# Keys, values and tables made ahead of the layers and behind V, in a two-layer hybrid decoder trunk

## What is computed

```python
for l in range(DEPTH):
    h = rmsnorm(x, norm_mix[l])
    ...   # projections; o_hg, o_s5, o_rt; gates; merge
    x = x + merged @ w_out[l]
    x = x + cross_attn(rmsnorm(x, norm_cross[l]), rmsnorm(mem, norm_mem[l]), xa_wq[l], xa_wkv[l], xa_wo[l])
    x = x + peer(rmsnorm(x, norm_ffn[l]), peer_wq[l], peer_keys[l], peer_u[l], peer_v[l])
# in cross_attn, mem_n = rmsnorm(mem, norm_mem[l]):
    k, v = jnp.split(mem_n @ wkv, 2, axis=-1)
# in s5, the tables: functions of the parameters alone
    dt = jnp.exp(log_step)[:, None]; mag = jnp.exp(lr * dt)
    a_re = mag * jnp.cos(li * dt); a_im = mag * jnp.sin(li * dt)
    bb_re = z_re[..., None] * b_re - z_im[..., None] * b_im
    bb_im = z_re[..., None] * b_im + z_im[..., None] * b_re
```

## Time and profile before

| | |
|---|---|
| median of 3 runs | 5575.65 us (5574.95 to 5576.41) |
| the profiled execution | 5575.93 us, its span 5574.1 us |
| TensorE busy | 4937.0 us, 89% of the span |
| VectorE busy | 2640.8 us, 47% |
| ScalarE busy | 1656.7 us, 30% |
| GpSimd busy | 290.5 us, 5% |
| DMA queue of SP | 717.58 MB, 39.1% of 16 engines' span |

### The profile page before, as it was taken

The page is one execution under the profiler, slowest core; times in us unless marked ns, Lnnn a source line. Parts: engine busy times, 40 slices in busy tenths (PEclk is TensorE's granted clock), DMA queues, the critical chain, the costliest instruction groups (busy, mean ns, idle before and its releaser), DMA issues. The chain is left out here.

```text
span 5574.1 us, 57335 instructions
## 1 busy us (share of the span) xinstructions
PE 4937.0 (89%) x23352; PEld 4085.8 (73%) x23352; DVE 2640.8 (47%) x4121; ACT 1656.7 (30%) x2116; POOL 290.5 (5%) x96
## 2 busy tenths in 40 slices
PE   7986387888999999999989765877799999999998
PEld 5765366666888888888877644665688888888887
DVE  2236743269744424444422466432796444244444
ACT  2232123232333322222232322232233333222222
POOL 0002300002100000000000122000030000000000
PEclk9998688998999999999999976888899999999999
DMA  2220032023455556666522101331144555566665
GB/s 109 91 95 16 12 132 98 31 80 118 136 189 183 182 170 192 199 188 197 170 107 95 76 16 23 121 113 46 50 135 151 181 176 183 183 186 199 192 193 164
DMA packets 308469, 721.24 MB, mean 129 GB/s; under 512 B 18544, under 2 KB 158576, under 8 KB 290672
## 3 DMA queue, kind: packets, MB, share of 16 engines
q1 hardware_dynamic: 308208, 717.58, 39.1%
HBM read 564.42 MB, written 148.90 MB: 128 GB/s over the span
## 5 line engine op out<-in xcount | busy, mean ns | idle before, releaser
L1629 PE MATMUL psum<-vl,ah 128*128 128x512 f32 x2048 | 796.7, 389 | 0.0
L1629 PE MATMUL psum<-vh,al 128*128 128x512 f32 x2048 | 796.7, 389 | 0.0
L1629 PE MATMUL psum<-vh,ah 128*128 128x512 f32 x2048 | 796.7, 389 | 0.0
L1718 DVE TENSOR_TENSOR ul<-u,uh 128x1024 fp32r<-128x1024 f32 x256 | 366.9, 1434 | 726.4 <-ACT uh L1655 724.0
L1797 DVE TENSOR_TENSOR vl<-v,vh 128x1024 fp32r<-128x1024 f32 x256 | 313.7, 1225 | 773.6 <-ACT vh L1686 773.6
L278 DVE TENSOR_TENSOR w_lo<-w,w_hi 128x1024 fp32r<-128x1024 f32 x232 | 282.6, 1225 | 834.1 <-ACT w_hi L273 833.6
L1595 PE MATMUL psum<-h_lo,uh 128*128 128x512 f32 x2048 | 518.2, 395 | 57.4 <-DVE ul L1718 57.4
L1686 ACT CAST vh<-v 128x1024 fp32r<-128x1024 f32 x256 | 268.3, 1048 | 977.7 <-PE psum L1629 962.3
L1595 PE MATMUL psum<-h_hi,ul 128*128 128x512 f32 x2048 | 508.9, 391 | 0.0
L1595 PE MATMUL psum<-h_hi,uh 128*128 128x512 f32 x2048 | 505.8, 389 | 0.0
L1595 PEld LDWEIGHTS psum<-h_lo,uh 128*128 128x128 f32 x2048 | 383.1, 190 | 135.4 <-DVE ul L1718 59.2
(11 more groups left out here) (410 smaller groups left out, 6516.3 us busy)
## 6 DMA issues: line engine op xcount, KB each, us to landing
u<-in_peer_u SPq DMA_DIRECT2D x256, 512.0 KB, 3.8
v<-in_peer_v SPq DMA_DIRECT2D x256, 512.0 KB, 3.7
gelu_of_dots<-ge SPq DMA_DIRECT2D x256, 256.0 KB, 2.1
gates_by_token<-held SPq DMA_DIRECT2D x32, 2048.0 KB, 7.6
act<-gelu_of_dots SPq DMA_DIRECT2D x64, 1024.0 KB, 7.0
gate<-gates_by_token SPq DMA_DIRECT2D x64, 1024.0 KB, 10.2
w<-in_w_fm SPq DMA_DIRECT2D x14, 2048.0 KB, 8.0
w<-in_w_gate SPq DMA_DIRECT2D x12, 2048.0 KB, 8.1
```

Of the source, the lines that this page charges most:

```text
L1629: mm = nc.tensor.matmul(psum[:, 2 * b + half, :], w[p][:, b * P:(b + 1) * P], q[p][:, half * W:(half + 1) * W], start=(n == 0 and x == 0), ...
L1718: v.tensor_tensor(fw(ul[r]), u[r][:], fw(uh[r]).bitcast(F32), ALU.subtract).then_inc(s["u_lo"], 1)
```

## The change

The keys and values of memory of both layers are made in one new stage, `memory_stage`, which stands behind the setup and a norm of memory for both gains, ahead of layer 0. They are written to DRAM and loaded back in the norm stage of each cross attention. The S5 tables are made by a class `TableWork`, by VectorE and ScalarE without GpSimd: those of layer 0 inside `memory_stage`, those of layer 1 inside the loop over V of layer 0. They too are written to DRAM (five stores, 7.6 MB), and `retention_stage` loads them back while it runs; it also zeroes the first part of `pc` on GpSimd. `ssm_tables_stage` and `load_small_stage` are gone; the small tables of both layers are loaded in the setup.

In `memory_stage` there are 32 units (per layer 8 of K, 8 of V). VectorE's part of the tables is two Python generators of steps; a step is one instruction or a few with a wait for its end. `first` gives one step behind each of units 0 to 5, `second` (88 steps) four behind each unit from 9 on. Behind V, `first` gives one step per tile from 6 on, `second` two per tile from 24 on; the five stores stand on SP behind the load of tile 116.

```diff
+    def __init__(self, sb, whole):
+        self.sin, self.cos, self.decay = (sb(n, [P, G5 * N5]) for n in ("tsin", "tcos", "tdec"))
+        self.gb = sb("gb", [P, G5, J5, C5])
+        if whole:
+            self.pc = sb("pc", [P, G5, 2 * J5, C5])
+            self.tail = self.pc[:, :, J5 - 1:, :]
+        else:
+            self.tail = sb("pc_tail", [P, G5, J5 + 1, C5])[:]
+    def parts(self, rest):
+        at = 0
+        for x in (self.sin, self.cos, self.decay):
+            yield x[:], rest[:, at:at + G5 * N5]
+            at += G5 * N5
+        for x, j in ((self.gb[:], J5), (self.tail, J5 + 1)):
+            n = j * C5
+            yield x.rearrange("p g j c -> p g (j c)"), rest[:, at:at + G5 * n].rearrange("p (g n) -> p g n", n=n)
+            at += G5 * n
...
+                 (m.cols[:], io["c_cols"]), (lbs[:], io["hgrn_lb"]), (mem[:], io["mem"])]
+        loads += [(m.small[:, l, :], tile_at(io["small"], l)) for l in range(L)]
...
+    outs = [(k, gain, dst) for k in range(KD) for gain, dst in zip(gains, dsts)]
...
+                for k, gain, (d_hi, d_lo) in outs:
...
+                for n, (part, rest) in enumerate(tabs.parts(m.tables_dram[l])):
+                    sp.dma_start(part, rest).then_inc(s["tables_in"], 16)
+                sp.wait_ge(s["tables_in"], 16 * (n + 1))
...
+                pool.memset(tabs.pc[:, :, 0:J5 - 1, :], 0.0).then_inc(s["zeros"], 1)
...
+class TableWork:
...
+    def load(self, sp):
+        sp.dma_start(self.bc[:].rearrange("p a g c -> p (a g c)"), tile_at(self.io["s5_bc"], self.l)).then_inc(self.s["bc_in"], 16)
+        sp.dma_start(self.nvec[:], self.io["c_nvec"]).then_inc(self.s["bc_in"], 16)
+    def store(self, sp):
+        sp.wait_ge(self.s["table_made"], 1)
+        for part, rest in self.tabs.parts(self.m.tables_dram[self.l]):
+            sp.dma_start(rest, part).then_inc(self.s["table_out"], 16)
+    def stored(self, sp):
+        sp.wait_ge(self.s["table_out"], 16 * 5)
...
+    def step_size(self, a):
+        a.wait_ge(self.s["bc_in"], 32)
+        a.activation(self.dt, self.col("log_step"), ACT.Exp).then_inc(self.s["dt_in"], 1)
+    def radii(self, a):
+        a.wait_ge(self.s["exp_in"], 1)
+        a.activation(self.mag, self.u1, ACT.Exp).then_inc(self.s["exp_done"], 1)
+        a.activation(self.r8, self.u1, ACT.Exp, scale=float(J5)).then_inc(self.s["exp_done"], 1)
+    def turns(self, a):
+        a.wait_ge(self.s["sin_in"], 1)
+        a.activation(self.aim, self.red, ACT.Sin).then_inc(self.s["sin_done"], 1)
+        a.activation(self.are, self.cred, ACT.Sin).then_inc(self.s["sin_done"], 1)
+    def sines(self, a):
+        a.wait_ge(self.s["tab_in"], 1)
+        a.activation(self.tabs.sin[:], self.tabs.sin[:], ACT.Sin, scale=TWO_PI).then_inc(self.s["tab_done"], 1)
+        a.activation(self.tabs.cos[:], self.tabs.cos[:], ACT.Sin, scale=TWO_PI).then_inc(self.s["tab_done"], 1)
...
+        yield st.link(v.tensor_copy(tabs.tail[:, :, 0, :], bc[:, 2]))
+        for h in range(2):
+            yield from self.combine(v, st, tabs.tail[:, :, 1:, :], self.pr[:, 1:, :], self.pi[:, 1:, :], 2, h, self.scratch[h][:])
+            yield from self.combine(v, st, tabs.gb, self.zr[:], self.zi[:], 0, h, self.scratch[h][:])
+    def last(self, v):
+        v.wait_ge(self.s["tab_done"], 2)
+        self.st.settle()
+        v.tensor_scalar(self.tabs.sin[:], self.tabs.sin[:], self.m.cols[:, 2:3], None, ALU.mult).then_inc(self.s["table_made"], 1)
...
+                pe.wait_ge(m.memory_in, 32 * (l + 1))
...
+                if work is not None:
+                    sp.wait_ge(s["dot_mm"], PK)
+                    work.load(sp)
...
+                    if work is not None and n == 116:
+                        work.store(sp)
+                if work is not None:
+                    work.stored(sp)
...
+                    if work is not None:
+                        if n == 4:
+                            work.step_size(a)
+                        elif n == 8:
+                            work.radii(a)
+                        elif n == 20:
+                            work.turns(a)
+                        elif n == 90:
+                            work.sines(a)
...
+                if work is not None:
+                    first, second = work.angles(v), work.powers_and_phases(v)
                 for n in range(2, PK):
                     low_v(n)
+                    if work is not None:
+                        if 6 <= n < 20:
+                            next(first, None)
+                        elif 24 <= n < 110:
+                            next(second, None)
+                            next(second, None)
+                        elif n == 110:
+                            work.last(v)
...
-def load_small_stage(nc, io, l, sm):
-    with stage(nc, "small_in") as s:
-        with nc.Block() as block:
-            @block.sync
-            def _(sp):
-                sp.dma_start(sm[:], tile_at(io["small"], l)).then_inc(s["small_in"], 16)
-                sp.wait_ge(s["small_in"], 16)
...
+                tabs = SsmTables(lambda n, sh: ctx.enter_context(buffer(nc, n, sh, F32)), True)
+                retention_stage(nc, m, l, part(fm, 3), part(fm, 4), part(fm, 5), part(tm, 1), part(fm, 4), tabs, psum, io)
...
+def memory_stage(nc, m, io, weights, acts, psum):
...
+                work.load(sp)
+                for t in range(2, len(kinds) + 2):
+                    if t < len(kinds):
+                        sp.wait_ge(s["lo_done"], 4 * (t - 1))
+                        weights.load(sp, t, t % 2)
+                    r = t - 2
+                    sp.wait_ge(s["copied"], behind[r + 1])
+                    rest = m.memory_dram[r // 4]
+                    if kinds[r] == "fm":
+                        sp.dma_start(rest[:, r % 2 * 4 * MEM:(r % 2 + 1) * 4 * MEM], made[r % 2][:]).then_inc(rested[r % 2], 16)
+                    else:
+                        sp.dma_start(rest[:, KD * MEM:].rearrange("p (b n) -> p b n", b=MB)[:, :, r % 2 * W:(r % 2 + 1) * W],
+                                     made[r % 2][:].rearrange("p (b n) -> p b n", b=MB)).then_inc(rested[r % 2], 16)
+                work.store(sp)
+                work.stored(sp)
+                for x in rested:
+                    sp.wait_ge(x, 16 * len(kinds) // 2)
...
+                    elif q == 3:
+                        a.wait_ge(s["unit_mm"], n + 1)
+                        for b in range(MB):
+                            a.copy(made[t % 2][:, b * W:(b + 1) * W], bank(t, b)).then_inc(s["copied"], 1)
+                work.step_size(a)
+                for n, (t, q) in enumerate(units):
+                    if q == 0:
+                        a.wait_ge(ready[t % 2], 16 * (t // 2 + 1))
+                    if n >= 2:
+                        a.wait_ge(s["unit_mm"], n - 1)
+                    a.copy(shaped(hi[n % 2], t), unit_of(t, q)).then_inc(s["hi_done"], 1)
+                    if n >= 2:
+                        copy_out(n - 2)
+                    if n == 3:
+                        work.radii(a)
+                    elif n == 7:
+                        work.turns(a)
+                    elif n == 28:
+                        work.sines(a)
+                copy_out(len(units) - 2)
+                copy_out(len(units) - 1)
+            @block.vector
...
+                first, second = work.angles(v), work.powers_and_phases(v)
+                for n, (t, q) in enumerate(units):
+                    v.wait_ge(s["hi_done"], n + 1)
+                    v.tensor_tensor(shaped(lo[n % 2], t), unit_of(t, q), shaped(hi[n % 2], t).bitcast(F32), ALU.subtract).then_inc(s["lo_done"], 1)
+                    if n < 6:
+                        next(first, None)
+                    elif n == 6:
+                        for _ in first:
+                            pass
+                    elif n >= 9:
+                        for _ in range(4):
+                            next(second, None)
+                for _ in second:
+                    pass
+                work.last(v)
...
+def memory_layers(nc, m, io, psum):
+    c = COL["norm_mem"][0]
+    tiles = [(io[name], 2 * l + t) for l in range(L) for name in ("xa_k", "xa_v") for t in range(2)]
+    with ExitStack() as ctx:
+        raw = two_tiles(nc, ctx)
+        weights = Weights(m, raw, 0, len(tiles), lambda t: tile_at(*tiles[t]))
+        acts = [ctx.enter_context(hi_lo(nc, f"memT{l}", [P, KD, MEM])) for l in range(L)]
+        with buffer(nc, "mem", [P, MB, D], F32) as mem:
+            setup_stage(nc, io, m, mem)
+            norm_stage(nc, m, mem, MB, [m.small[:, l, c:c + KD] for l in range(L)], acts, psum, weights)
+        memory_stage(nc, m, io, weights, acts, psum)
...
-        w_k, w_v, w_q, w_o = (Weights(m, raw, i + 1, 2, lambda t, name=name: tile_at(io[name], l * 2 + t))
-                              for i, name in enumerate(("xa_k", "xa_v", "xa_q", "xa_o")))
-        c = COL["norm_mem"][0]
```

(26 more changed lines are left out.)

372 lines of the change are left out of this document (195 added, 177 removed).

## The result

The changed kernel took 5442.59 us in the median (5437.63 to 5458.39, 4 runs), the kernel before 5575.3 (5572.88 to 5576.41, 4 runs): 0.9767 of the time, 95% interval 0.9755 to 0.9779, 132.7 us less. Forecast were 115 us less, 5461, with a range from 5437 to 5492. The profiled execution is the slowest of the four, 5458.39 us with a span of 5456.6, 117.5 less than that of the kernel before.

What follows compares the result with a forecast made beforehand. TensorE was taken as the bound wherever it multiplies, so the gain lay in its idle time or removable work. Terms: -329.7 + 183.2 + 29.7 + 1.8 = -115.0 us, from 5575.9 to 5461; range 5437 to 5492.

Steps and rivals of the forecast that it cites:

- What goes: Both layers: tables stages 182.7 us, memory part of the cross layers 143.7, load of small tables 3.3; 329.7 gone.
- 182.7 less 1.8: Tables stages gone, 182.7 us, less 1.8 in retention, where GpSimd's memset comes before its first product, 0.9 per layer.
- The front stage: Ahead of layer 0: norm of memory 14.3 us, stage with units, tables and storing 168.6, setup 0.3; 183.2 added.
- the 2 of the last unit: Front stage: the last unit starts at the lower clock, 2 us more, beside 42.4 for the tables.
- The 2.5 us for a lower clock at the beginning: Front stage: first products after an idle stretch run at a lower granted clock, 2.5 us more.
- Behind V: Layer 0: tables 14.3 us, slow start 1.9, late load of V's tile 2 1.5, store 12; 29.7 added.
- the final products: Behind V: 6.9 us in each of four units overflow by 13.5; with phases 14.3, and 1.9 for a slow start.
- the store: Behind V: the tables' store delays the load of tile 117, a stall of 10 us and 2 for the slow start.
- Rival 2: Store behind V hidden, loads and stores sharing the engines: 12 us less, 5449; chance 0.10.
- Rival 3: Front stage: weaving costs more than the steps, 16 units at 1 us each, +16; 5477 to 5490, chance 0.17.
- Rival 5: Slower than before: retention waits at its end for the tables' loads; 5600 if they took 120 us; chance 0.03.
- rival 1: Whole kernel: everything as priced, with bounds of store rate, lower clock and stall; 5448 to 5476, chance 0.62.

Runs made afterwards that it cites:

- The run with memory alone: Kernel before with keys and values of memory and small tables made ahead of the layers, tables stage left behind retention with GpSimd: 5542.69 us, 0.9939 of before.
- apart: Changed kernel with one difference behind V each: final products one step each, one step per tile from 64, 5432.38 us; five stores singly behind five tiles, 5433.49 us.
- both kernels with the tables stage in its old place: Kernel before with VectorE alone making pc and gb, 5548.78 us; kernel before with only the memory part moved ahead of the layers, 5542.69 us.
- both filled: Kernel before and changed kernel, each with five unused TensorE products in the gap ahead of the state-space stage's small products: 5555.45 and 5437.43 us.
- the filling: Five unused 128x512 products in that gap, added to kernel before, 5555.45 us; changed kernel, 5437.43; changed kernel with spread products, single stores and even front stage, 5377.09.

## Why the prediction was right

*What goes.* 329.7 us by the sum. The two stretches with the memory parts gave back 147.1 (forecast 143.7). From the load behind the mixer to that of the output weights alone it is 72.1 and 71.8, 143.9, so the forecast of this term is met; the other 3.2 us lie ahead of it, from the gates to the end of the mixer, 2.4 of them in layer 0, and why is open. The two tables stages with retention gave back 179.8 (forecast 180.9, which is 182.7 less 1.8).

*The front stage.* 183.2 forecast, 180.9 measured. The terms came out: copies, stores and leaving took 22.6 us, 184.47 to 207.11, for 23.4. The last product ended at 184.5, 138.7 us behind the first cast for 140 in the sum. The run with memory alone needs 94.8 for the same units, so what the tables add is 43.9, for 42.4 and the 2 of the last unit. The 2.5 us for a lower clock at the beginning were not due (granted 1.00 from 45.69 to 60.00, also with memory alone), and near the last two units it was low (0.61 to 0.66 from 165 to 186), as the sum had it.

*Behind V.* 29.7 forecast, 30.0 measured; apart, the final products cost 14.0 to 16.7 (14.3 + 1.9 = 16.2 in the sum, with the phases and the slow start) and the store 10.8 to 13.3 (12). That the whole agrees within 0.3 us is in part luck: idle time was 22.0 us where the sum has 25.8 (14.3 + 1.5 + 10), mostly since the four gaps near tile 66 were 10.3 together and not 13.5, and the lower clock cost 8.0 where the sum has 3.9 (1.9 + 2). The mechanism is the predicted one, the split of its price was not. Rival 2, the store hidden, is out by the landing of 20.3 us. Rival 3 is out as well: in the front, ten units with four steps each followed one another at 2.82 us (71.11 to 99.31), and at 2.80 in the run without table work. Rival 5: retention took 53.4 us in layer 0 (678.7 to 732.1) where 53.1 were needed before, and its loads of tables lay beside it. (The 10.2 us for 1 MB in small pieces, "at the latest" in the prediction, are a median; nothing hung on them.)

*What the forecast did not have.* The median stands 18 us under the forecast, inside the range but below the 5448 at which the bounds of rival 1, the forecast, begin, and nearer to the 5449 of rival 2, which the trace rules out; by its number alone the median would have spoken for the wrong rival. Some 15 us of this are the granted clock in the state-space stage. The step of the sum that did not hold is a silent one: the sum took for granted that a stage that isn't touched takes what it took. The small products ran at 0.50 in both layers in the profiles of the kernel before and of both kernels with the tables stage in its old place. With the stage moved they run at 1.00 in some runs and layers, 10 us less each. Like with like (both filled), the change is worth 5555.45 - 5437.43 = 118.0 us, and the forecast of 115 is its size; the last 14.7 of the 132.7 are the clock's. What decides in a given run is not settled. The length of the gap does not: over all profiles without the filling the lower clock followed gaps of 1.58 to 2.32 us, and the clock stayed at 1.00 behind gaps of 1.65 to 2.14. The place of the tables stage has to do with it: with the stage in its old place every profile has both layers at 0.50, and the 28 runs of the kernel before, three sets of 9 to 10, lie between 5572.7 and 5578.9, while with the stage moved any of the three levels comes. By what it does so is open. The filling removed the lower clock from all three profiles taken with it.

## What to carry to other kernels

Work woven into another engine's spare time is free piece by piece and dear in lumps: spread it so that no tile gets more than its spare time, by the durations of the trace; the same twelve instructions cost 14 to 17 us in four lumps, and one by one they opened no gap. A store on the queue that feeds the inner loop is paid by the next load: split it, send each part as it is ready, and look for stores held back by an older entry of the same queue. Before a change of a few tenths of a per cent is judged, look at the granted clock of stages that were not touched, and compare profiles at the same level there.

## What the hardware showed unexpectedly

A gap of about 2 us on TensorE in front of small products (64 columns) was followed, in some profiles, by the lower clock from some 3 us on to the end of them, so that they took 24 us instead of 14, and whether it was so varied between runs of one kernel. The Trainium skill (TensorE: Matmul & The Clock Gate, What's actually happening) says that how many products run at the lower clock at the start of a kernel varies from run to run; the traces show such a variation in the middle of one, with a difference of 10 us per layer.

Stores from SBUF to DRAM, with every engine idle, moved 435 GB/s, and so did the stores and the loads of V together near tile 117 (windows of the changed kernel):

```profile
190.00:204.00 14.00, 0.00 (x0) 0.00 (x0) 0.00 (x0) 0.00 (x0) 0.00 (x0) 0.50 1.03 435
2756.00:2768.00 12.00, 9.68 (x43) 7.69 (x41) 2.40 (x3) 0.46 (x1) 0.00 (x0) 1.00 1.02 435
```

The Trainium skill (DMA: Bandwidth & Descriptors, Where 436 GB/s comes from) has about 358 GB/s bind between HBM and SBUF; the measurement decides, and it is the higher figure here.
